# Strassen blocks in the feed-forward of a two-layer trunk, one weight sum of each block made by an adding DMA

## The chip, the core and the metric

One core of one Trainium2 chip runs the whole program. The time is the device time of one launch in microseconds, and of several launches the median. Engines are called as in the profile: PE is TensorE (PEld its weight loads), DVE is VectorE, ACT is ScalarE, POOL is GpSimd, SP is SyncE, which issues nearly all DMAs.

## What is computed

Two layers over 256 rows of 1024 numbers, all in float32. Each layer is a half-step SwiGLU feed-forward, a mixer (convolution branch, latent attention, gates, one output projection), and a second half-step feed-forward. The change is in the feed-forward, of which the program holds four (two in each layer):

```python
D_MODEL = 1024; SEQ = 256; DEPTH = 2; D_FF = 2816
def _swiglu(h, w_gate, w_up, w_down):
    return (jax.nn.silu(h @ w_gate) * (h @ w_up)) @ w_down
...
    for l in range(DEPTH):
        x = x + 0.5 * _swiglu(_rms_norm(x, ffn1_norm[l]), ffn1_w_gate[l], ffn1_w_up[l], ffn1_w_down[l])
        h = _rms_norm(x, mix_norm[l])
        ...
        x = x + y @ w_out[l]
        x = x + 0.5 * _swiglu(_rms_norm(x, ffn2_norm[l]), ffn2_w_gate[l], ffn2_w_up[l], ffn2_w_down[l])
    return x
```

## The kernel before, in words

**Split operands.** PE works on fp32r operands, and each float32 operand is kept as two of them: a rounded part ("hi") and what the rounding left ("lo"). A product is three matmuls (`products`, L663 to L665): hi by hi, hi by lo, lo by hi. For a weight block, ACT makes the hi part (`split` on ACT, L1123, raw to whi) and DVE the lo part (`split` on DVE, L1517, raw minus whi to wlo).

**Units.** Weights come in units of 128 by 2048 numbers (1 MB). `raw` holds three of them as they land, `whi` and `wlo` hold six (RING). SP loads a unit with two DMAs (`place`) when DVE has made the lo part of the unit three places earlier, ACT splits it when PE has released the unit six places earlier (`unit_free`), DVE follows ACT (`whi_ready`), and PE waits for DVE (`wlo_ready`). GpSimd takes DVE's part in a stretch of the mixer.

**Feed-forward.** The 2816 hidden columns are cut in 11 chunks of 256. For chunk c, `gate_up(c, t)` multiplies the 128 rows of tile t by 256 gate and 256 up columns side by side, over 8 blocks of 128 inner rows: 24 matmuls of 128x512 for each of two tiles, from two units. ACT applies silu to the gate half (L1216), DVE multiplies by the up half (`mul`, L1623) into `gu`. This must be transposed for the down product: ACT sorts the 32-bit words into 16-bit planes (`split_planes`, L1225), SP issues a DMA transpose (`plane_turn`, L402), DVE joins the planes again (`join`, L1636) into `g_turned`, ACT rounds that to gThi (`round_joined`, L1233) and DVE makes gTlo (`rest_joined`, L1522). Then `down(c, t)` adds chunk c to the output with 12 matmuls for each tile, from one unit, and waits for gTlo (`glo`). PE's order is gate_up(c), down(c-2), so a chunk is 72 matmuls. Chunks 4 and later run in a hardware loop on PE, chunks 2 and later on ACT and DVE.

**What sets the order.** Each engine runs the list that is written out for it, in order, and waits on semaphores. Nothing is moved by a scheduler. An instruction that waits holds up all that is written behind it on its engine, and SP's DMAs too are issued in the written order.

**GpSimd** computes inverse roots for the norms (`root`, L531) and, once in each layer, the angles for the rotary positions (L549 to L588, 36 counted steps), which ACT needs at the start of the mixer (L1321).

## Time and profile before

| | |
|---|---|
| median of 3 runs | 1047.45 us (1047.15 to 1047.8) |
| span of the profiled execution | 1045.7 us |
| PE busy | 1040.6 us |
| DVE, ACT, POOL busy | 687.1, 593.7, 248.9 us |
| granted TensorE clock | 1.000, the upper of its two levels |
| DMA | 208.81 MB, mean 200 GB/s |

The span is 1.75 us below the median of the times. In the page, the busy time of each engine tells which is always at work, the digits by slice tell whether that changes along the span, and the chain that ended last names the engine whose work the end waited for. A start and a duration in a timeline row overlap with the next row by some 0.1 us, since an engine begins an instruction while the one before it drains. So the cost of one instruction in a row of many is the distance between two starts.

### The profile page before, as it was taken

Reading aid. Unit: us, or ns where it says so; the run is one execution under the profiler, and the core shown is the slowest. Engines: PE = TensorE matmul, PEld = TensorE weight load, DVE = VectorE, ACT = ScalarE, POOL = GpSimd, SP = SyncE. Lnnn points to the kernel's source line nnn. Section 1 sums busy time; section 2 is a strip of 40 time slices with the busy share of each in tenths; the row PEclk is TensorE's granted clock in tenths of the full one; section 3 lists DMA queues with packets and bytes.
Section 4 is the critical chain, followed back from the end, with each engine's and each line's share of the span. In section 5 each row is a group of like instructions: output and inputs, shape, how many; then the busy total and the mean of one; then the engine's idle time right before and its main releaser. Section 6 shows DMA issues by size and latency. Waiting matters only on the chain.

```text
span 1045.7 us, 13767 instructions
## 1 busy us (share of the span) xinstructions
PE 1040.6 (100%) x5001; PEld 872.2 (83%) x5001; DVE 687.1 (66%) x911; ACT 593.7 (57%) x792; POOL 248.9 (24%) x258
## 2 busy tenths in 40 slices
PE   9999999999999999999999999999999999999998
PEld 6888888998888888888888888889988888888887
DVE  6755655698976766555576555656999677656551
ACT  6754544576874665445466454536778557645440
POOL 2960000148850000000048300002588300000000
PEclk9999999999999999999999999999999999999999
DMA  8977666455644696675569667565366366976641
GB/s 280 310 237 234 186 211 200 143 200 172 210 163 125 206 313 188 206 232 196 153 191 282 216 206 228 184 199 172 122 212 224 118 191 222 261 221 186 207 139 41
DMA packets 191555, 208.81 MB, mean 200 GB/s; under 512 B 64112, under 2 KB 162704, under 8 KB 191504
## 3 DMA queue, kind: packets, MB, share of 16 engines
q1 hardware_dynamic: 190288, 206.03, 63.6%
q10 hardware_dynamic: 1216, 2.11, 0.7%
q8 instruction: 31, 0.51, 0.2%
q14 instruction: 20, 0.16, 0.1%
HBM read 192.90 MB, written 1.05 MB: 185 GB/s over the span
## 4 chain that ended last, share of the span: by engine, by line
PE 98%; ACT 1%; DVE 1%; issue 0%; POOL 0%; ACTq 0%
PE bank L663 31%; PE bank L665 31%; PE bank L664 31%; PE bank L744 1%; PE bank L905 1%; PE bank L914 1%; PE bank L935 1%; PE bank L670 1%; PE bank L702 0%; PE bank L913 0%; PE bank L937 0%; DVE htok L1563 0%; DVE x L1611 0%; ACT htok L1132 0%; PE bank L923 0%; PE bank L963 0%
## 5 line engine op out<-in xcount | busy, mean ns | idle before, releaser
L1517 DVE TENSOR_TENSOR wlo<-raw,whi 128x2048 fp32r<-128x2048 f32 (+2 forms) x152 | 347.4, 2290 | 82.6 <-ACT whi L1123 81.5
L663 PE MATMUL bank<-whi,hThi 128*128 128x512 f32 (+1 forms) x976 | 378.4, 388 | 0.0
L665 PE MATMUL bank<-whi,hTlo 128*128 128x512 f32 (+1 forms) x976 | 373.7, 383 | 0.0
L664 PE MATMUL bank<-wlo,hThi 128*128 128x512 f32 (+1 forms) x976 | 373.6, 383 | 0.0
L1123 ACT ACTIVATE whi<-raw 128x2048 fp32r<-128x2048 f32 (+2 forms) x176 | 335.3, 1910 | 16.8 <-DMA raw<-in_ffn_w_up 7.3
L665 PEld LDWEIGHTS bank<-whi,hTlo 128*128 128x128 f32 x976 | 183.3, 188 | 35.7
L663 PEld LDWEIGHTS bank<-whi,hThi 128*128 128x128 f32 x976 | 183.4, 188 | 35.1 <-issue 0.3
L664 PEld LDWEIGHTS bank<-wlo,hThi 128*128 128x128 f32 x976 | 183.4, 188 | 34.8
L1216 ACT ACTIVATE gates<-bank,small 128x256 f32<-128x256 f32 x88 | 41.8, 475 | 263.5 <-PE bank L665 262.8
L663 PE MATMUL bank<-whi,gThi 128*128 128x512 f32 (+1 forms) x416 | 162.2, 390 | 0.0
L664 PE MATMUL bank<-wlo,gThi 128*128 128x512 f32 (+1 forms) x416 | 161.1, 387 | 0.0
L665 PE MATMUL bank<-whi,gTlo 128*128 128x512 f32 (+1 forms) x416 | 161.1, 387 | 0.0
L531 POOL TENSOR_TENSOR small<-small,expo 128x1 f32<-128x1 f32 (+3 forms) x20 | 24.2, 1214 | 566.3 <-DVE small L1556 529.5
L1623 DVE SCALAR_TENSOR_TENSOR gates<-bank,small,gates 128x256 f32<-128x256 f32 x88 | 42.4, 483 | 168.1 <-ACT gates L1216 168.0
L645 POOL TENSOR_TENSOR wlo<-raw,whi 128x2048 fp32r<-128x2048 f32 x24 | 110.2, 4612 | 21.9 <-ACT whi L1123 21.9
L1717 DVE SCALAR_TENSOR_TENSOR bank<-cu,vec,bank 128x256 f32<-128x256 f32 x240 | 98.1, 479 | 0.2
L665 PEld LDWEIGHTS bank<-whi,gTlo 128*128 128x128 f32 x416 | 78.1, 188 | 16.0
L663 PEld LDWEIGHTS bank<-whi,gThi 128*128 128x128 f32 x416 | 78.1, 188 | 15.8 <-issue 0.4
L664 PEld LDWEIGHTS bank<-wlo,gThi 128*128 128x128 f32 x416 | 78.2, 188 | 15.5
L1225 ACT ACTIVATE qkT<-gates 128x512 uint16<-128x512 uint16 x80 | 49.5, 620 | 0.0
L549 POOL TENSOR_TENSOR small<-expo 128x1 f32<-128x1 f32 x72 | 36.5, 507 | 5.9
L663 PE MATMUL bank<-hThi,whi 128*128 128x256 f32 x128 | 36.4, 284 | 0.0
(177 smaller groups left out, 823.6 us busy)
## 6 DMA issues: line engine op xcount, KB each, us to landing
raw<-in_ffn_w_down SPq DMA_DIRECT2D x88, 512.0 KB, 4.2
raw<-in_ffn_w_gate SPq DMA_DIRECT2D x84, 512.0 KB, 4.3
raw<-in_ffn_w_up SPq DMA_DIRECT2D x84, 512.0 KB, 5.4
raw<-in_w_in SPq DMA_DIRECT2D x48, 512.0 KB, 4.8
raw<-in_w_out SPq DMA_DIRECT2D x16, 512.0 KB, 4.4
raw<-in_w_in SPq DMA_DIRECT2D x8, 544.0 KB, 4.5
raw<-in_w_mla_out SPq DMA_DIRECT2D x8, 512.0 KB, 3.9
raw<-in_w_conv_out SPq DMA_DIRECT2D x8, 512.0 KB, 4.7
```

The source lines that it names most:

```text
L531: return nc.gpsimd.tensor_tensor(out, in_, expo[:, :].to_broadcast([P, out.shape[-1]]), ALU.pow)
L549: nc.gpsimd.tensor_tensor(small[:, 95:96], expo[:, :], expo[:, :], ALU.mult)
L645: nc.gpsimd.tensor_tensor(wlo[:, slot(u, RING), 0:n], raw[:, slot(u, RAW), 0:n], whi[:, slot(u, RING), 0:n].bitcast(F32), ALU.subtract).th ...
L663: nc.tensor.matmul(out, lh, rh, start=start, stop=False, skip_group_check=skip)
L664: nc.tensor.matmul(out, lh, rl, start=False, stop=False, skip_group_check=skip)
L665: return nc.tensor.matmul(out, ll, rh, start=False, stop=stop, skip_group_check=skip)
L1123: nc.scalar.activation(whi[:, slot(u0, RING), 0:USED[u0]], raw[:, slot(u0, RAW), 0:USED[u0]], ACT.Copy).then_inc(whi_ready, 1)
L1216: nc.scalar.activation(sgate[:, t, :], gu_bank(c, t)[:, 0:FC], ACT.Silu, scale=rs[:, t:t + 1]).then_inc(silu_ready, 1)
L1225: nc.scalar.activation(planes[:, :, :, t, :], words, ACT.Copy).then_inc(planes_ready, 1)
L1517: nc.vector.tensor_tensor(wlo[:, slot(u0, RING), 0:n], raw[:, slot(u0, RAW), 0:n], whi[:, slot(u0, RING), 0:n].bitcast(F32), ALU.subtract) ...
L1623: nc.vector.scalar_tensor_tensor(out=gu[:, t, :], in0=gu_bank(c, t)[:, FC:2 * FC], scalar=rs[:, t:t + 1], in1=sgate[:, t, :], op0=ALU.mult ...
L1717: ins = nc.vector.scalar_tensor_tensor(out=o, in0=i, scalar=w, in1=o, op0=ALU.mult, op1=ALU.add)
```

## The change

In each feed-forward, the chunks 3 and 4, and the chunks 6 and 7, form a block (BLK). A block is a product of a 2 by 2 matrix (row tiles t by inner halves h) with a 2 by 2 matrix (inner halves by gate and up, each 512 columns wide). It is computed with seven products of 12 matmuls in place of eight, by Winograd's form of Strassen's method. The products are called by their right operand: B11, T1, T2, B22, B21, T3, T4. The left operands are hT itself or one of four sums of its quarters (`mixed_rows`), made and split once in each feed-forward into sThi and sTlo. The right operands are the quarters of the weights or sums of them:

- `chain[0]` (in `htok`) is loaded by SP with the upper half of gate, which is B11. DVE adds to it three times, 128x2048 each: the upper half of up (`add_T1`, gives T1), the lower half of up (`add_T2`, gives T2), the lower half of gate (`add_T4`, gives T4). B22 and B21 are those lower halves of up and gate, loaded into `raw`.
- T3 is made in `chain[1]` (in `heads`): SP loads the upper half of up there, and an adding DMA issued by GpSimd (`add_rows`) adds the lower half of up from memory, in two parts of 512 KB.

The PSUM results are combined in `kept`: ACT copies four (`keep`), DVE makes four combinations of 128x512 (`up_first`, `gate_first`, `up_second`, `gate_second`), ACT applies silu twice at 128x512 and DVE multiplies twice at 128x512. Each of the seven right operands is a unit in the ring of six, with a hi part from ACT and a lo part from DVE, so that two chunks have 7 + 2 such splits where they had 4 + 2. The plain chunks stay as they were, but all loops are written out. `gain`, `bias`, `vtok` and `cu` of the mixer now share their room with sThi and sTlo, and `g_turned` has moved into `gates`. The core of the diff:

```diff
+BLK = (3, 6)
+PRODUCTS = ("B11", "T1", "D0", "T2", "B22", "B21", "T3", "T4", "D1")
...
+            def chain_load(l, f, c, i):
...
+                for k in (0, 2):
+                    sp.dma_start(dst[:, k:k + 2, :], src[:, k:k + 2, :]).then_inc(chain_landed[i], 16)
...
+            def add_rows(l, f, c):
+
+                done = per_block(l, f, c)
+                pool.wait_ge(chain_landed[1], done * 32)
+                pool.wait_ge(sum_ready, (done - 1) * 3 + 1)
...
+                for k in (0, 2):
+                    nc.gpsimd.dma_start(dst[:, k:k + 2, :], src[:, k:k + 2, :], accum_op=ALU.add).then_inc(added_landed, 16)
...
             for l in range(DEPTH):
                 norm(l, 0)
+                for c in BLK:
+                    add_rows(l, 0, c)
...
+                def block_product(c, name, b, lhs, start=True, stop=True):
+
+                    u = unit_block(f, c, name)
+                    unit_waits(pe, l, u)
+                    for k in range(4):
+                        ins = products(bank[:, b, :], lhs(k), wt(u, 2048, 4, k, slice(0, CW)),
+                                       start=start and k == 0, stop=stop and k == 3, skip=True)
+                    ins.then_inc(unit_free, 1)
...
+                    block_product(c, "B11", 4, plain_T(0, 0))
...
+                    block_product(c, "T1", 5, mixed_T(1, 1))
+                    down(c - 2, 0)
+                    down(c - 2, 1)
...
+                    block_product(c, "T2", 4, mixed_T(0, 0), start=False)
...
+                    block_product(c, "B22", 5, mixed_T(1, 0), start=False)
...
+                    block_product(c, "B21", 6, plain_T(1, 0))
...
+                    block_product(c, "T3", 4, mixed_T(0, 1), start=False)
...
+                    block_product(c, "T4", 7, plain_T(1, 1))
+                    down(c - 1, 0)
+                    down(c - 1, 1)
...
                 first()
-                pair(2, 2)
-                pair(3, 3)
-                with pe.Fori(0, (NCH - 5) // 2) as i:
-                    pair(i * 2 + 4, 4)
-                    pair(i * 2 + 5, 5)
+                pair(2)
+                strassen(3)
+                pair(5)
+                strassen(6)
+                pair(8)
+                pair(9)
                 last()
...
+                def mixed_round():
+
+                    act.wait_ge(mix_step, (l * 2 + f + 1) * 5)
+                    nc.scalar.activation(sThi[:, :, :], mixed, ACT.Copy).then_inc(mixed_hi, 1)
...
+                def add(c, i, other):
+
+                    nc.vector.tensor_tensor(chain[i], chain[i], other, ALU.add).then_inc(sum_ready, 1)
```

**VectorE at the start of the second feed-forward.** Before, from its third weight split on (L1517 the split, L1623 `mul`, L1636 `join`, L1522 `rest_joined`):

```order
L1517 TENSOR_TENSOR wlo<-raw,whi 128x2048 [waits whi_ready]
L1623 SCALAR_TENSOR_TENSOR gates<-bank,small,gates 128x256 [waits rs_ready,silu_ready]
L1517 TENSOR_TENSOR wlo<-raw,whi 128x2048 [waits whi_ready] x2
L1623 SCALAR_TENSOR_TENSOR gates<-bank,small,gates 128x256 [waits planes_ready,silu_ready]
L1636 COPY vtok<-qkT 128x2x512 [waits turned_landed]
L1517 TENSOR_TENSOR wlo<-raw,whi 128x2048 [waits whi_ready]
L1522 TENSOR_TENSOR gTlo<-vtok,gThi 128x512 [waits ghi]
L1623 SCALAR_TENSOR_TENSOR gates<-bank,small,gates 128x256 [waits planes_ready,silu_ready]
L1517 TENSOR_TENSOR wlo<-raw,whi 128x2048 [waits whi_ready]
```

The same place now, from the first row that is new, in two pieces (L2021 the sums of hT, L1854 a weight split, L1978 `join`, L1963 `mul`, L1861 `rest_joined` or the split of the sums, L2001 `add_T1` and `add_T2`):

```order
L2021 TENSOR_TENSOR gates<-hThi,hTlo 128x2048 [waits nlo,nhi]
L1963 SCALAR_TENSOR_TENSOR gates<-bank,small,gates 128x256 [waits planes_ready,silu_ready]
L2021 TENSOR_TENSOR gates<-gates 128x4x128 [waits mix_step]
L2021 TENSOR_TENSOR gates<-gates 128x4x128
L2021 TENSOR_TENSOR gates<-gates 128x4x128 [waits mix_step] x2
L1854 TENSOR_TENSOR wlo<-raw,whi 128x2048 [waits whi_ready]
L1978 COPY gates<-qkT 128x2x512 [waits turned_landed]
L1963 SCALAR_TENSOR_TENSOR gates<-bank,small,gates 128x256 [waits planes_ready,silu_ready]
L1861 TENSOR_TENSOR gTlo<-gates,gThi 128x512 [waits ghi]
```

```order
L1854 TENSOR_TENSOR wlo<-htok,whi 128x2048 [waits whi_ready]
L2001 TENSOR_TENSOR htok<-htok,heads 128x2048 [waits chain_landed1]
L1963 SCALAR_TENSOR_TENSOR gates<-bank,small,gates 128x256 [waits planes_ready,silu_ready]
L1861 TENSOR_TENSOR sTlo<-gates,sThi 128x2048 [waits mixed_hi]
L1963 SCALAR_TENSOR_TENSOR gates<-bank,small,gates 128x256 [waits planes_ready,silu_ready]
L1854 TENSOR_TENSOR wlo<-htok,whi 128x2048 [waits whi_ready]
L1978 COPY gates<-qkT 128x2x512 [waits glo,turned_landed]
L2001 TENSOR_TENSOR htok<-htok,raw 128x2048 [waits raw_landed1]
L1861 TENSOR_TENSOR gTlo<-gates,gThi 128x512 [waits ghi]
L1854 TENSOR_TENSOR wlo<-raw,whi 128x2048 [waits whi_ready]
```

Between two `mul` rows stood one or two weight splits. Now there stand the sums of hT, the adds and the split of the sums beside them, and the last row is the lo part of D1, the unit that `down(1)` needs.

**ScalarE at the same place.** Before (L1225 planes, L1123 weight split, L1216 silu, L1233 `round_joined`):

```order
L1225 ACTIVATE qkT<-gates 128x4x128 [waits gu_ready]
L1123 ACTIVATE whi<-raw 128x2048 [waits unit_free,raw_landed2]
L1216 ACTIVATE gates<-bank,small 128x256 [waits gu_done]
L1123 ACTIVATE whi<-raw 128x2048 [waits unit_free,raw_landed0]
L1233 ACTIVATE gThi<-vtok 128x512 [waits joined]
L1225 ACTIVATE qkT<-gates 128x4x128 [waits turned_landed,gu_ready]
L1216 ACTIVATE gates<-bank,small 128x256 [waits unit_free]
```

and now (L1503 planes, L1350 weight split, L1447 silu, L1511 `round_joined`, L1495 `mixed_round`):

```order
L1447 ACTIVATE gates<-bank,small 128x256 [waits gu_done]
L1350 ACTIVATE whi<-htok 128x2048 [waits unit_free,chain_landed0]
L1503 ACTIVATE qkT<-gates 128x4x128 [waits turned_landed,gu_ready]
L1511 ACTIVATE gThi<-gates 128x512 [waits joined]
L1495 ACTIVATE sThi<-gates 128x2048 [waits mix_step]
L1447 ACTIVATE gates<-bank,small 128x256 [waits unit_free]
L1503 ACTIVATE qkT<-gates 128x4x128 [waits gu_ready]
L1350 ACTIVATE whi<-htok 128x2048 [waits unit_free,sum_ready]
L1447 ACTIVATE gates<-bank,small 128x256 [waits gu_done]
```

The silu of chunk 1, tile 1 now stands behind `round_joined(0)` and `mixed_round`, and the silu of chunk 2, tile 0 behind the hi part of T1, which waits for `add_T1`.

**SyncE at the same place.** Before, the first transpose of a chunk (L402) stood right behind the loads of one down unit:

```order
L377 DMA raw<-in_ffn_w_gate 128x4x256 [waits wlo_ready]
L377 DMA raw<-in_ffn_w_up 128x4x256
L377 DMA raw<-in_ffn_w_down 128x1024 [waits wlo_ready]
L377 DMA raw<-in_ffn_w_down 128x1024
L402 DMA_TRANSPOSE qkT<-qkT 128x8x128 [waits joined,planes_ready]
```

and now:

```order
L469 DMA raw<-in_ffn_w_down 128x1024 [waits wlo_ready]
L469 DMA raw<-in_ffn_w_down 128x1024
L498 DMA htok<-in_ffn_w_gate 128x2x512 [waits sq_ready]
L498 DMA htok<-in_ffn_w_gate 128x2x512
L469 DMA raw<-in_ffn_w_down 128x1024 [waits wlo_ready]
L469 DMA raw<-in_ffn_w_down 128x1024
L498 DMA heads<-in_ffn_w_up 128x2x512 [waits block_joined1]
L498 DMA heads<-in_ffn_w_up 128x2x512
L469 DMA raw<-in_ffn_w_up 128x2x512 [waits wlo_ready]
L469 DMA raw<-in_ffn_w_up 128x2x512
L522 DMA_TRANSPOSE qkT<-qkT 128x8x128 [waits joined,planes_ready]
```

Five units (D0, chain[0], D1, chain[1], B22) are issued between the last unit of chunk 2 and the transpose of chunk 0, where one was.

## Rows read from the trace of the kernel before

**Rows 1.** The page: engines, busy by slice, and the chain that ended last

```profile
PE 1040.6 (100%) x5001; PEld 872.2 (83%) x5001; DVE 687.1 (66%) x911; ACT 593.7 (57%) x792; POOL 248.9 (24%) x258
PE   9999999999999999999999999999999999999998
PE 98%; ACT 1%; DVE 1%; issue 0%; POOL 0%; ACTq 0%
```

**Rows 2.** Timeline, ScalarE, second feed-forward: start, us, engine, line, instruction, [idle before]

```profile
353.64 1.97 ACT L1123 ACTIVATE whi<-raw 128x2048 fp32r<-128x2048 f32 x1
355.45 0.67 ACT L1225 ACTIVATE qkT<-gates 128x512 uint16<-128x512 uint16 x1
357.04 0.47 ACT L1216 ACTIVATE gates<-bank,small 128x256 f32<-128x256 f32 x1 [0.92 <-PE bank L665]
357.41 1.91 ACT L1123 ACTIVATE whi<-raw 128x2048 fp32r<-128x2048 f32 x1
...
360.14 1.92 ACT L1123 ACTIVATE whi<-raw 128x2048 fp32r<-128x2048 f32 x1 [0.30 <-DMA raw<-in_ffn_w_up]
...
373.36 0.47 ACT L1216 ACTIVATE gates<-bank,small 128x256 f32<-128x256 f32 x1 [0.69 <-PE bank L665]
...
378.80 0.47 ACT L1216 ACTIVATE gates<-bank,small 128x256 f32<-128x256 f32 x1 [1.41 <-PE bank L665]
```

**Rows 3.** Timeline, VectorE, same stretch

```profile
352.44 2.29 DVE L1517 TENSOR_TENSOR wlo<-raw,whi 128x2048 fp32r<-128x2048 f32 x1 [0.67 <-ACT whi L1123]
354.65 0.48 DVE L1623 SCALAR_TENSOR_TENSOR gates<-bank,small,gates 128x256 f32<-128x256 f32 x1
...
355.64 2.29 DVE L1517 TENSOR_TENSOR wlo<-raw,whi 128x2048 fp32r<-128x2048 f32 x1 [0.45 <-ACT whi L1123]
357.85 0.48 DVE L1623 SCALAR_TENSOR_TENSOR gates<-bank,small,gates 128x256 f32<-128x256 f32 x1
...
364.70 0.75 DVE L1636 COPY vtok<-qkT 128x1024 uint16<-128x1024 uint16 x1
365.33 2.28 DVE L1517 TENSOR_TENSOR wlo<-raw,whi 128x2048 fp32r<-128x2048 f32 x1
```

**Rows 4.** The page's groups: plain weight splits and the operations of 128x512 on each engine

```profile
L1517 DVE TENSOR_TENSOR wlo<-raw,whi 128x2048 fp32r<-128x2048 f32 (+2 forms) x152 | 347.4, 2290 | 82.6 <-ACT whi L1123 81.5
L1522 DVE TENSOR_TENSOR gTlo<-vtok,gThi 128x512 fp32r<-128x512 f32 x40 | 27.4, 686 | 3.3 <-ACT gThi L1233 3.3
L1233 ACT ACTIVATE gThi<-vtok 128x512 fp32r<-128x512 f32 x40 | 24.9, 622 | 18.1 <-DVE vtok L1636 17.6 <-PE bank L665 0.5
```

**Rows 5.** Timeline, SyncE's queue, second feed-forward

```profile
354.76 0.37 SPq L377 DMA_DIRECT2D raw<-in_ffn_w_gate  x1
355.17 0.51 SPq L377 DMA_DIRECT2D raw<-in_ffn_w_up  x1
357.96 0.82 SPq L377 DMA_DIRECT2D raw<-in_ffn_w_down  x2
359.86 1.23 SPq L402 DMA_TRANSPOSE qkT<-qkT  x1
```

**Rows 6.** The page: DMA issues, KB each, median us from issue to landing

```profile
raw<-in_ffn_w_gate SPq DMA_DIRECT2D x84, 512.0 KB, 4.3
raw<-in_ffn_w_up SPq DMA_DIRECT2D x84, 512.0 KB, 5.4
```

**Rows 7.** Two transposes by themselves: behind a down unit's loads at 37.0, behind none

```profile
L402 SPq DMA_TRANSPOSE qkT<-qkT x1: 1232/1232/1232, 37.0 to 37.0; - x1
...
DMA to landing us min/median/max: 5.1/5.1/5.1
...
L402 SPq DMA_TRANSPOSE qkT<-qkT x1: 1232/1232/1232, 62.8 to 62.8; - x1
...
DMA to landing us min/median/max: 3.0/3.0/3.0
```

**Rows 8.** By window: us, busy of PE, PEld, DVE, ACT, POOL, clock, DMA share, GB/s

```profile
22.30:72.90 50.60, 50.60 (x224) 41.72 (x223) 35.91 (x29) 32.39 (x34) 45.53 (x88) 1.00 1.00 293
...
26.00:52.00 26.00, 26.00 (x116) 21.33 (x115) 20.40 (x16) 18.76 (x19) 23.77 (x37) 1.00 1.11 313
...
346.00:400.00 54.00, 54.00 (x244) 44.83 (x243) 37.62 (x37) 36.64 (x42) 0.57 (x1) 1.00 0.79 240
```

**Rows 9.** Timeline, GpSimd: two angle steps of layer 1, then first and last of layer 0

```profile
578.56 2.14 POOL L549 TENSOR_TENSOR small<-expo 128x1 f32<-128x1 f32 x1
...
580.76 2.35 POOL L568 TENSOR_SCALAR ang<-ang 128x32 f32<-128x32 f32 x1
...
23.70 11.63 POOL L556 TENSOR_SCALAR ang<-small 128x2 f32<-128x2 f32 x16
...
67.51 0.20 POOL L549 TENSOR_TENSOR small<-expo 128x1 f32<-128x1 f32 x1
...
72.29 0.57 POOL L549 TENSOR_TENSOR small<-expo 128x1 f32<-128x1 f32 x1
```

**Rows 10.** Timeline, VectorE, beside the first two of rows 9

```profile
578.35 4.62 DVE L1517 TENSOR_TENSOR wlo<-raw,whi 128x2048 fp32r<-128x2048 f32 x2 [1.23 <-ACT whi L1123]
```

**Rows 11.** Timeline, ScalarE: where layer 0's mixer takes the angles

```profile
202.31 0.34 ACT L1321 ACTIVATE cossin<-ang 128x32 f32<-128x32 f32 x2
```

More of the change, by code:

```diff
@@ L61 @@
 UM = U_FFN
-assert U_LAYER % RING == 0 and U_LAYER % RAW == 0
+assert U_LAYER % RING == 0
+LOADED = [u for f in range(2) for u in range(UB[f], UB[f] + U_FFN)
+          if FFN_UNITS[u - UB[f]][0] in ("G0", "G1", "D", "B22", "B21")] + list(range(UM, UM + U_MIX))
+LOADED.sort()
+R_LAYER = len(LOADED)
+PLAIN = [c for c in range(NCH) if not any(b <= c < b + 2 for b in BLK)]
 M_PR, M_C01, M_UQ, M_UKV, M_C23, M_G, M_MLA, M_CO, M_WO = 0, 2, 4, 5, 6, 8, 16, 18, 20
@@ L808, in turn, with down @@
                     ins.then_inc(gtr, 1)
-                def down(c, c0, t, last=False, between=None):
+                def down(c, t, last=False, between=None):
                     pe.wait_ge(glo, per_ffn(l, f, c, t))
@@ new lines, in ffn @@
+                silu(1, 0)
+                first_of(3, "B11")
+                split_planes(1, 0)
+                round_joined(0)
+                mixed_round()
+                silu(1, 1)
+                split_planes(1, 1)
+                sum_of(3, "T1")
+                silu(2, 0)
+                down_split(1)
+                split_planes(2, 0)
+                silu(2, 1)
+                round_joined(1)
+                split_planes(2, 1)
+                block_first(3)
+                block_second(3)
@@ new lines, in ffn @@
+                    gate_split(2, 0)
+                    gate_split(2, 1)
+                    mul(0, 1)
+                whole_rows()
+                mul(1, 0)
+                mixed_rows()
+                down_split(0)
+                join(0)
+                mul(1, 1)
+                rest_joined(0)
+                of_chain(3, "B11")
+                add_T1(3)
+                mul(2, 0)
+                mixed_rest()
+                mul(2, 1)
+                of_chain(3, "T1")
+                join(1)
@@ new lines, in ffn @@
+                add_T2(3)
+                rest_joined(1)
+                down_split(1)
+                of_chain(3, "T2")
+                add_T4(3)
+                join(2)
+                lower(3, "B22")
+                lower(3, "B21")
+                rest_joined(2)
+                of_chain(3, "T3")
+                of_chain(3, "T4")
+                block_second(3)
+                of_chain(6, "B11")
+                add_T1(6)
+                join(3)
+                rest_joined(3)
+                mul(5, 0)
@@ new lines, in ffn @@
+                of_chain(6, "T1")
+                join(4)
+                add_T2(6)
+                mul(5, 1)
+                rest_joined(4)
+                down_split(4)
+                of_chain(6, "T2")
+                add_T4(6)
+                lower(6, "B22")
+                join(5)
+                lower(6, "B21")
+                rest_joined(5)
+                of_chain(6, "T3")
+                of_chain(6, "T4")
+                block_second(6)
+                gate_split(9, 0)
+                join(6)
```

588 lines of the change are left out of this document (445 added, 143 removed).

## The prediction

> **What bounds the kernel now.** I read the engines' busy time first, then the chain that ended last, then the timelines of one feed-forward. PE is busy for 1040.6 of 1045.7 us, at nine tenths or more in all slices but the last, and it is 98% of the chain [rows 1]. So fewer matmuls make the kernel faster, as long as nothing that PE waits for gets later than its lead. From one silu of ScalarE to the next of the same chunk lie one tile's 24 matmuls: 378.80 - 373.36 = 5.44 us [rows 2], or 0.2267 us for a matmul of 128x512. In that stretch VectorE is busy for 37.6 of 54 us and ScalarE for 36.6 [rows 8].
>
> **What is removed.** Each block takes 7 x 12 matmuls where two chunks took 96. That is 12 fewer, 8 blocks, 96 x 0.2267 = **21.8 us** off PE. All of it lies on the path.
>
> **What is added on VectorE.** A split of 128x2048 costs 2.21 us from start to start (352.44 to 354.65), `mul` 0.40, `join` 0.63 (364.70 to 365.33) [rows 3]; an operation of 128x512 lasts 0.686 [rows 4], less some 0.08 of overlap 0.61. The trace has no add of two SBUF tiles, but the split is such an operation, with two SBUF inputs of the same size and another operator. I take 2.21 for an add (bounds 2.2 and 2.3). A block has 3 more splits and 3 adds, 13.3 us, and the combinations (4 x 0.61) and two wide for four narrow multiplies (1.22 - 1.60) bring it to 15.3. Two blocks and the sums of hT (2.21 + 4 x 0.61 + 2.21 = 6.9) make 37.5 us more in each feed-forward. ScalarE gets 3 more splits of 1.81 (353.64 to 355.45 [rows 2]) and four copies of about 0.52 (0.622 long [rows 4]) in each block, and one more split for the sums.
>
> On the average this fits. A block lasts 144 - 12 = 132 matmuls, 29.9 us, and VectorE's work in it is 9 x 2.21 + 3 x 2.21 + 2.4 + 1.2 + 2 x (0.63 + 0.61) = 32.6 us, while a plain chunk leaves it 16.3 - 8.7 = 7.6 us free. The ring of six units carries the lack of 2.7 us. The question is the order, and the tightest place is the first block of a feed-forward.
>
> **The walk to D1.** I use the clock of the trace in the second feed-forward [rows 2, 3, 5]; the lists are those in the section on the change. Up to VectorE's second split the lists agree. The split of the second unit of chunk 2 can't begin before 362.0: its load is issued when the first split has ended (354.76 [rows 5]) and it lands at 360.1, where ScalarE takes it today too [rows 2]. That split ends at 364.2, and `mul(0,1)`, done today at 358.2 [rows 3], at 364.6. From there VectorE has until D1's lo part is done: three adds or sums of 2.21 (the whole of hT, `add_T1`, `add_T2`), four of 0.61, the split of the sums, three splits (D0, B11, T1), and D1's (together 8 x 2.21 = 17.7), 2.4, four `mul` 1.6, two joins and two rests 2.5. That is 24.2 us, and ends at 388.8.
>
> PE comes to D1 at 378.8 (end of chunk 2) + 5.44 (down(0)) + 2 x 2.72 (B11, T1) = **389.7**. So without any wait VectorE would be there 0.9 us ahead. It has these waits, each a wait for ScalarE or a DMA that stands in line:
> - `mul(1,0)` for its silu, which ScalarE reaches behind D0's hi part: 0.6.
> - `join(0)` for the transpose. VectorE comes to it at 372.6. The transpose is issued at about 365.5 behind five units, 5.24 MB, whose issue begins at 358.0. The second DMA of a unit is issued 0.41 us after the first [rows 5] and lands 5.4 - 4.3 = 1.1 us later after its own issue [rows 6], so 524 KB take 1.5 us, 350 GB/s; over 26 us the queue moved 313 GB/s at a full share [rows 8]. 5.24 MB at 350 take 15 us from about 360.2. The transpose waits for loads ahead of it: 5.1 us with one down unit before it against 3.0 with none [rows 7]. It lands at 375.5, and VectorE waits 2.9. Bounds: 0 if transposes pass loads, 5 at 313 GB/s.
> - `mul(1,1)` for its silu, which now stands behind `round_joined(0)` (0.52) and `mixed_round` (1.81): with hand-overs 2.8.
> - `mul(2,0)` for its silu, behind T1's hi part, which waits for `add_T1`: 1.81 + 0.35 = 2.2. PE had those products done long before.
> - four small hand-overs, 0.4 in all.
>
> Together 8.9 us, so D1 is ready at 388.8 + 8.9 = 397.7, **8.0 us** after PE wants it. PE meets them in pieces: 1.2 at down(0), 1.7 at B11 (bank 4 is free only after `mul(2,0)`), 2.1 at T1, 3.0 at D1. Behind D1, VectorE stays ahead: T2, `add_T4`, join, B22 end at 405.0, and PE, with D1 from 397.7, wants T2 at 403.1 and B22 at 405.9.
>
> **The rest of a feed-forward.** VectorE ends T4 at 412.2 (after B21, a rest and T3). From there to the end of `rest_joined(3)` it has 6 x 2.21 + 7 x 0.61 + 0.63 = 18.2 us of work, and waits of 3.7: `up_second` for a `keep` that stands behind a silu (1.3), the second multiply for a silu behind D3's hi part (1.3), B11 (0.4), the round (0.7). That is 434.1. PE ends T4 at 403.1 + 5 x 2.72 = 416.7 and wants down(3) at 416.7 + 5.4 + 10.9 = 433.0: **1 us** late. To the second block's T4 VectorE has some 41 us of work for PE's 204 matmuls, 46.2 us, and stays ahead. Then the transpose of chunk 6 stands in SyncE's list behind both units of chunk 9, the second of which waits for the second split of chunk 8; I have it issued 1.7 us into gate_up(8). From there: 5.5 to land (between the two of rows 7 and more), two `split_planes` and a round on ScalarE 1.6, the hi and lo parts of chunk 9's second unit 1.8 + 2.2, since `rest_joined(6)` stands behind them, that rest 0.6: 13.4 us after gate_up(8) began, which lasts 10.9: **2.5 us** late. In the first feed-forward the queue is already full (share 1.11 [rows 8]), so `join(0)` waits some 2.5 us longer.
>
> **The sum.** 1045.7 - 21.8 + 4 x (8.0 + 1.0 + 2.5) + 2.5 = 1072.4, against the profile's own span. The median lies 1.75 above the span, so I predict **1074 us**, slower by 2.5%.
>
> The Trainium skill (DMA: Bandwidth & Descriptors, Queues, rings and completion order) says that each engine consumes the descriptors of one queue in ring order, and that another queue is served in turns. The transpose rows agree. By it the adding DMA, on GpSimd's queue, slows the transposes but doesn't stand before them, and the sum stays as it is.
>
> **What else moves and costs nothing.** The memset of `cu` (128x120) and the later load of `gain` lie under matmuls with slack of tens of us. The loops written out bring more instruction loads, in a queue with 0.2% of the DMA engines' time. The clock stood at its upper level throughout [rows 8]; I leave it there, as waits of 1 to 3 us between runs of matmuls are short.
>
> **Rivals.**
> 1. *VectorE keeps its lead.* If the hand-overs on ScalarE are covered and the transpose passes the loads, PE sees next to nothing, and the time is 1047.5 - 21.8 = 1025.7 to 1035. For it: the free 0.9 us of the walk, and the 7.6 us free in each plain chunk. Against: the two silus stand in ScalarE's list behind the waits, and no speed of DMA removes those 5.0 us.
> 2. *Only the queue is better than I think.* Without the wait for `join(0)` and with quick transposes the first block is 5.1 late, and chunks 3 and 6 together about 0.5, as the transpose is some 2 us sooner: 4 x 5.6 = 22 against 21.8, so 1048, within 1041 to 1053.
> 3. *The adding DMA, or GpSimd behind it, is late.* ScalarE needs T3's sum some 17 us after `add_T1`, VectorE 21 us after; the two plain loads of a unit take 5.9 (0.5 of issue and 5.4 [rows 6]). So the adding DMA decides when it is more than about three times slower than a load, and then each us costs one in each of 8 blocks: at 5 us over, 1074 + 40 = 1114. No row shows an adding DMA. The same engine starts the angles only after the second block's add, at about 106 us, not 23.7 [rows 9]. A GpSimd operation of 0.20 us lasts 2.14 beside a split, and of two splits back to back each lets one operation through [rows 9, 10]. The angles are 88 instructions [rows 8] from 23.7 to 72.9; where nothing holds them, 18 take 72.29 - 67.51 = 4.8 us [rows 9], so all take 23.5. Some 25 splits and adds between 106 and the mixer, 55 us, and 23.5 of their own end at 185, against ScalarE's need at 202.3 [rows 11] plus delays. It holds, with little room, and would cost 5 to 15 us in each layer if not.
>
> The Trainium skill (SBUF — State Buffer, Who interferes with whom) has this as a rule: a VectorE instruction with two SBUF inputs contends with a GpSimd instruction that reads SBUF, and the later one blocks. The trace agrees (2.14 against 0.20).
>
> **How the numbers follow.** The forecast (PE waits 9 to 16 us in each feed-forward) has 0.61 and its own range of 1058 to 1090; rival 2 has 0.14, rival 1 0.13, rival 3 0.12. The range of 1041 to 1098 leaves out rival 1 and half of rival 3, 0.19. A measurement of this kernel can tell 0.2% (2 us) from no change. Faster: rival 1 and 0.07 of rival 2, 0.20. The same: 0.05. Slower: 0.75.
>
> **What would show it.** Right: PE idle 10 to 13 us in each feed-forward, with waits at the down products of chunks 0, 3 and 6, at B11, T1 and D1 of the first block; VectorE idle before `join(0)` and before the multiplies of chunks 1 and 2, "released by ACT gates"; transposes that land 8 to 10 us after issue; PE busy about 1019. Wrong: transposes of 3 us beside queued loads, or VectorE with no gap before those rows; an adding DMA of over 17 us; ScalarE waiting for `added_landed` or for the angles.

## The result, and the profile after

| | before | after |
|---|---|---|
| median, us | 1047.3 (1047.02 to 1047.8, 4 runs) | 1089.66 (1085.8 to 1090.2, 4 runs) |
| span of the profiled execution | 1045.7 | 1088.4 |
| PE busy | 1040.6 | 1041.4 |
| PE idle (span less busy) | 5.1 | 47.0 |
| granted clock, mean | 1.00 | 0.984 |

The changed kernel takes 1.0398 times as long (95% interval 1.0386 to 1.0411): 42.4 us more, where the forecast was 26.7 more. The page has these engines, and this clock in 40 slices:

```profile
PE 1041.4 (96%) x4905; PEld 863.9 (79%) x4905; DVE 830.4 (76%) x1000; ACT 660.1 (61%) x836; POOL 293.7 (27%) x274
PEclk9899999999999999999999999999999999899999
```

PE has the 96 matmuls fewer (against [rows 1]), and yet it is as busy as before. The list of waits shows the idle time (engine, line, waited for: us in total, times, longest):

```profile
PE bank L833 <- DVE gTlo L1861: 22.2, 10, 3.2
PE bank L833 <- DVE wlo L1854: 15.8, 8, 2.7
PE bank L833 <- DVE gates L1963: 2.9, 2, 1.5
```

These three rows are 40.9 us, and all of it is released by VectorE: lo parts of gated values (at the down products), lo parts of weights (at T1 and D1), multiplies (at B11). What else the list has is 2.3 us, nearly all of it in the first 13 us of the program. PE's timeline of the second feed-forward has the six places one by one, with the wait at the end of the row; in order they are the down products of chunk 0, B11, T1, D1, and the down products of chunks 3 and 6:

```profile
393.02 0.50 PE L833 MATMUL bank<-whi,gThi 128*128 128x512 f32 x1 [1.37 <-DVE gTlo L1861]
400.25 0.50 PE L833 MATMUL bank<-whi,hThi 128*128 128x512 f32 x1 [1.46 <-DVE gates L1963]
405.22 0.47 PE L833 MATMUL bank<-whi,sThi 128*128 128x512 f32 x1 [1.96 <-DVE wlo L1854]
410.86 0.47 PE L833 MATMUL bank<-whi,gThi 128*128 128x512 f32 x1 [1.06 <-DVE wlo L1854]
448.38 0.50 PE L833 MATMUL bank<-whi,gThi 128*128 128x512 f32 x1 [1.89 <-DVE gTlo L1861]
497.68 0.64 PE L833 MATMUL bank<-whi,gThi 128*128 128x512 f32 x1 [2.76 <-DVE gTlo L1861]
```

What the forecast did not have stands behind the last of these waits. PE's timeline (start, duration):

```profile
494.52 0.39 PE L835 MATMUL bank<-whi,hTlo 128*128 128x512 f32 x1
497.68 0.64 PE L833 MATMUL bank<-whi,gThi 128*128 128x512 f32 x1 [2.76 <-DVE gTlo L1861]
...
500.67 0.63 PE L834 MATMUL bank<-wlo,gThi 128*128 128x512 f32 x1
501.10 0.49 PE L835 MATMUL bank<-whi,gTlo 128*128 128x512 f32 x1
501.43 0.40 PE L833 MATMUL bank<-whi,gThi 128*128 128x512 f32 x1
501.66 0.40 PE L834 MATMUL bank<-wlo,gThi 128*128 128x512 f32 x1
```

From start to start a matmul takes 0.43 us here, and from 501.43 on 0.23 again. There are eight such stretches in the trace. By window (us, busy of PE, clock, DMA share, GB/s), four of them:

```profile
48.80:54.30 5.50, 5.50 (x15) 0.51 0.25 48
405.80:409.20 3.40, 3.40 (x10) 0.51 0.82 118
497.70:501.40 3.70, 3.70 (x9) 0.54 0.84 255
949.70:955.20 5.50, 5.50 (x14) 0.50 0.54 194
```

The granted clock is at its lower level, 1.2 GHz, for 3 to 6 us of matmuls each time. I took the time between the starts of neighbouring matmuls over the whole trace behind the start of the program and summed what exceeds 0.2267 us. In gaps over 0.5 us that is 46.2 us: 22 waits, two of them under 0.25 us, and four intervals right behind a wait, in which the first matmul at the lower clock took 0.54 to 0.59 us (1.4 us in all, so a part of the clock's price stands among the waits). In intervals of 0.3 to 0.5 us it is 22.2 us, against 6.6 in the trace before: **15.6 us of slow matmuls**. So 1045.7 - 21.8 + 46.2 + 15.6 = 1085.7 of the 1088.4. Of the 2.7 left, 1.3 is ahead of the first wait (PE starts the same matmul at 39.6 us before and at 40.9 now), and 1.4 I can't assign.

### The profile page after: what moved, and what is told of

It is laid out like the page before. It is cut to its first block and busy times, and to the rows that moved or that the text cites. A ratio compares the mean times of both kernels' runs of the same rounds, so it can differ in the third digit from the quotient of the medians.

```text
span 1088.4 us, 13247 instructions
## 1 busy us (share of the span) xinstructions
PE 1041.4 (96%) x4905; PEld 863.9 (79%) x4905; DVE 830.4 (76%) x1000; ACT 660.1 (61%) x836; POOL 293.7 (27%) x274
## 5 line engine op out<-in xcount | busy, mean ns | idle before, releaser
L1854 DVE TENSOR_TENSOR wlo<-raw,whi 128x2048 fp32r<-128x2048 f32 (+2 forms) x136 | 308.9, 2283 | 50.8 <-ACT whi L1350 50.6
L1350 ACT ACTIVATE whi<-raw 128x2048 fp32r<-128x2048 f32 (+2 forms) x160 | 303.1, 1910 | 48.5 <-DMA raw<-in_ffn_w_up 34.4
L833 PE MATMUL bank<-whi,hThi 128*128 128x512 f32 (+1 forms) x816 | 316.5, 388 | 2.9 <-DVE gates L1963 2.9
L835 PE MATMUL bank<-whi,hTlo 128*128 128x512 f32 (+1 forms) x816 | 311.4, 382 | 0.0
L834 PE MATMUL bank<-wlo,hThi 128*128 128x512 f32 (+1 forms) x816 | 311.3, 382 | 0.0
L833 PE MATMUL bank<-whi,gThi 128*128 128x512 f32 (+1 forms) x416 | 170.0, 409 | 31.5 <-DVE gTlo L1861 22.2
L833 PEld LDWEIGHTS bank<-whi,hThi 128*128 128x128 f32 x816 | 153.3, 188 | 32.6 <-DVE gates L1963 4.1
L835 PEld LDWEIGHTS bank<-whi,hTlo 128*128 128x128 f32 x816 | 153.2, 188 | 29.8
L1503 ACT ACTIVATE qkT<-gates 128x512 uint16<-128x512 uint16 x80 | 49.3, 626 | 102.9 <-DMA qkT<-qkT 45.6
L2212 DVE SCALAR_TENSOR_TENSOR bank<-shared,vec,bank 128x256 f32<-128x256 f32 x240 | 98.1, 479 | 0.2
L1350 ACT ACTIVATE whi<-htok 128x2048 fp32r<-128x2048 f32 x32 | 61.1, 1910 | 21.7 <-DVE htok L2001 21.3
L1854 DVE TENSOR_TENSOR wlo<-htok,whi 128x2048 fp32r<-128x2048 f32 x32 | 73.0, 2282 | 1.2 <-ACT whi L1350 1.2
L1963 DVE SCALAR_TENSOR_TENSOR gates<-bank,small,gates 128x256 f32<-128x256 f32 x56 | 26.9, 481 | 55.2 <-ACT gates L1447 55.0
```

The costliest lines, as they stand in the source:

```text
L833: nc.tensor.matmul(out, lh, rh, start=start, stop=False, skip_group_check=skip)
L834: nc.tensor.matmul(out, lh, rl, start=False, stop=False, skip_group_check=skip)
L835: return nc.tensor.matmul(out, ll, rh, start=False, stop=stop, skip_group_check=skip)
L1350: nc.scalar.activation(whi[:, slot(u, RING), 0:USED[u]], src, ACT.Copy).then_inc(whi_ready, 1)
L1503: nc.scalar.activation(planes[:, :, :, t, :], words, ACT.Copy).then_inc(planes_ready, 1)
L1854: nc.vector.tensor_tensor(wlo[:, slot(u, RING), 0:n], src, whi[:, slot(u, RING), 0:n].bitcast(F32), ALU.subtract).then_inc(wlo_ready, 1)
```

## The experiments

"Waits" in this table is the span less PE's busy time, "slow" the excess of intervals of 0.3 to 0.5 us over the 6.6 of before. Medians are of 4 runs, and of 10 to 12 for loops_out and where the text says five rounds. The 2.6 of busy_waits, at a clock of 1.00, is the first interval behind each run of zeros, 0.33 us long.

| kernel | median | span | waits | slow | clock |
|---|---|---|---|---|---|
| before | 1047.3 | 1045.7 | 5.1 | 0 | 1.00 |
| changed | 1089.7 | 1088.4 | 47.0 | 15.6 | 0.984 |
| loops_out | 1047.4 | 1045.6 | 6.5 | 0 | 1.00 |
| waits_put_in | 1085.5 | 1083.4 | 33.6 | 7.7 | 0.987 |
| busy_waits | 1082.2 | 1081.2 | 17.7 | 2.6 | 1.00 |
| silu_first | 1076.2 | 1077.5 | 40.2 | 12.6 | 0.986 |
| rests_first | 1073.1 | 1071.7 | 38.2 | 10.5 | 0.989 |
| both_orders | 1063.7 | 1061.0 | 31.8 | 7.0 | 0.991 |
| fill_b11 | 1053.9 | 1051.9 | 25.4 | 5.1 | 0.995 |
| third_silu | 1047.0 | 1044.4 | 17.7 | 7.0 | 0.993 |
| third_busy | 1045.9 | 1043.2 | 8.0 | 0.9 | 1.00 |
| room_made | 1048.3 | 1041.7 | 18.3 | 2.8 | 0.998 |
| sum_on_vector | 1105.4 | 1103.1 | 59.6 | 18.4 | 0.981 |
| turn_queue | 1088.9 | 1086.5 | 45.4 | 18.1 | 0.983 |

### The slow matmuls: is it PE's waiting, the longer program, or something else?

> The kernel before with its three loops over chunks written out, as the changed kernel has them, and nothing else. Theory (the 16 us that my forecast lacked are matmuls at the lower clock behind PE's waits): no wait, no change, 1045 to 1050 us, granted clock 1.00. Rival (the longer program itself costs, by instruction loads): 1055 to 1063 us.

```
-                with pe.Fori(0, (NCH - 5) // 2) as i:
-                    pair(i * 2 + 4, 4)
-                    pair(i * 2 + 5, 5)
+                for c in range(4, NCH - 1):
+                    pair(c, c)
...
```

The loops of ScalarE and VectorE are written out in the same way. 1047.36 us, ratio 1.0002 (0.9993 to 1.0012): the written-out loops cost nothing.

> The kernel before with its loops written out and ten waits of PE put in: in each of the two second feed-forwards PE waits, ahead of the down products of five chunks, for a chain of 2, 4, 6, 9 and 12 small operations on GpSimd that begins when the products ahead have ended. At some 0.5 us for an operation the waits are about 1, 2, 3, 4.5 and 6 us, 33 us in all. Theory (a wait of PE of some 3 us brings its clock down for the matmuls behind it, whatever the cause of the wait): the granted clock falls behind the longer waits and stands at 1.00 behind the shortest, and the time is the kernel before plus the waits plus 1.3 to 2.6 us for each wait of 3 us and more, 1088 to 1096 us. Rival (the slow matmuls of the changed kernel have another cause than its waits): clock 1.00 throughout, time the kernel before plus the waits alone, 1080 us.

```
+HOLDS = ((3, 2), (5, 4), (6, 6), (8, 9), (9, 12))
...
+                for i, (c, n) in enumerate(HOLDS):
+                    unit_released(pool, l, unit_gu(1, c, 1))
+                    for j in range(n):
+                        held[0] += 1
+                        nc.gpsimd.tensor_tensor(small[:, 95:96], expo[:, :], expo[:, :], ALU.mult).then_inc(hold_step, 1)
+                        pool.wait_ge(hold_step, held[0])
+                    pool.sem_inc(hold_done, 1)
...
+                    if f == 1 and c in [h for h, _ in HOLDS]:
+                        pe.wait_ge(hold_done, l * len(HOLDS) + [h for h, _ in HOLDS].index(c) + 1)
                     down(c - 2, c0 - 2, 0)
```

1085.54 us (ratio 1.0369, 1.0352 to 1.0387). The waits came out at 0.65, 1.20, 1.75, 2.57 and 7.7 us, twice each. This is PE's timeline around a wait of 2.57, and then the windows behind waits of 0.65, 1.75, 2.57 and 7.7:

```profile
1018.38 0.50 PE L676 MATMUL bank<-whi,gThi 128*128 128x512 f32 x1 [2.57 <-POOLq L668]
1018.72 0.55 PE L677 MATMUL bank<-wlo,gThi 128*128 128x512 f32 x1
1019.07 0.63 PE L678 MATMUL bank<-whi,gTlo 128*128 128x512 f32 x1
```

```profile
930.60:934.00 3.40, 3.40 (x16) 1.00 0.77 284
983.00:986.00 3.00, 3.00 (x14) 1.00 0.84 280
1018.60:1022.00 3.40, 3.40 (x9) 0.53 0.86 189
1045.00:1049.50 4.50, 4.50 (x12) 0.50 0.02 4
```

The clock fell behind all four waits of 2.57 us and more, and behind none of the six shorter ones. There is no Strassen block in this kernel, so a wait is enough. 30.5 us of gaps and 7.7 of slow matmuls are the 38.2 us by which it is longer than loops_out. The time is 2.5 us below the range that I gave: the waits came out 2.5 us shorter in all than the 33 us expected, and four of them were long enough for a fall, where I had six.

> The changed kernel, with products of zeros put ahead of the places where PE waits (8 ahead of the down products of chunk 0, 6 ahead of B11, 8 ahead of T1, 6, 7 and 11 ahead of the down products of chunks 1, 3 and 6), so that PE works in about the time in which it waited. They add zero, and nothing else is changed. Theory (idle PE brings the clock down): the clock stays at 1.00 or near it, the runs of 7 to 13 matmuls at 0.42 us are gone, and the time is 1088 less about 14 us, plus 1 to 4 for zeros that last longer than the wait they fill: 1073 to 1080 us. Rival (the clock falls for another reason): the slow runs stay, 1087 to 1094 us.

```
                     else:
+                        stay_busy(6)
                         pe.wait_ge(gu_ready, per_gu(l, f, 2, 0))
                     block_product(c, "B11", 4, plain_T(0, 0))
...
                     else:
+                        stay_busy(8)
                         pe.wait_ge(gu_ready, per_gu(l, f, 2, 1))
...
+                    if t == 0 and c == 0:
+                        keep_busy(8)
+                    elif t == 0 and c in (1, 3, 6):
+                        stay_busy({1: 6, 3: 7, 6: 11}[c])
                     pe.wait_ge(glo, per_ffn(l, f, c, t))
```

1082.18 us, clock 1.00. In PE's timeline the zeros stand where the waits were:

```profile
390.76 1.90 PE L840 MATMUL bank<-zero 128*128 128x512 bf16 x8
392.68 0.50 PE L833 MATMUL bank<-whi,gThi 128*128 128x512 f32 x1
...
398.26 1.47 PE L845 MATMUL bank<-zero 128*128 128x512 bf16 x6
399.90 0.50 PE L833 MATMUL bank<-whi,hThi 128*128 128x512 f32 x1 [0.18 <-DVE gates L1975]
```

Two zeros more last 1.90 - 1.47 = 0.43 us, so the 184 take 39.6. PE's other busy time is 1063.5 - 39.6 = 1023.9, against 1041.4 in the changed kernel: 17.5 us less, and every stretch of slow matmuls is gone. The gain in time is only 7.5 us, 2 short of the range I gave, since the zeros and the waits left (39.6 + 17.7 = 57.3) last 10.3 us longer than the 47.0 of waits that they replace. The rival is out. PE's idle time brings the clock down, and not the products of the blocks.

### The waits: what stands in line ahead of what VectorE needs?

VectorE's timeline in the changed kernel has the waits that the prediction named, ahead of `join(0)`, `mul(1,1)` and `mul(2,0)`; ScalarE's shows why, and SyncE's queue the transpose:

```profile
383.55 2.29 DVE L1854 TENSOR_TENSOR wlo<-raw,whi 128x2048 fp32r<-128x2048 f32 x1
388.20 0.76 DVE L1978 COPY gates<-qkT 128x1024 uint16<-128x1024 uint16 x1 [2.36 <-DMA qkT<-qkT]
391.88 0.48 DVE L1963 SCALAR_TENSOR_TENSOR gates<-bank,small,gates 128x256 f32<-128x256 f32 x1 [2.92 <-ACT gates L1447]
...
399.71 0.48 DVE L1963 SCALAR_TENSOR_TENSOR gates<-bank,small,gates 128x256 f32<-128x256 f32 x1 [2.34 <-ACT gates L1447]
```

```profile
388.26 0.63 ACT L1503 ACTIVATE qkT<-gates 128x512 uint16<-128x512 uint16 x1 [5.86 <-DMA qkT<-qkT]
389.05 0.63 ACT L1511 ACTIVATE gThi<-gates 128x512 fp32r<-128x512 f32 x1 [0.16 <-DVE gates L1978]
389.59 1.90 ACT L1495 ACTIVATE sThi<-gates 128x2048 fp32r<-128x2048 f32 x1
391.40 0.45 ACT L1447 ACTIVATE gates<-bank,small 128x256 f32<-128x256 f32 x1
...
397.40 1.91 ACT L1350 ACTIVATE whi<-htok 128x2048 fp32r<-128x2048 f32 x1 [4.37 <-DVE htok L2001]
399.22 0.45 ACT L1447 ACTIVATE gates<-bank,small 128x256 f32<-128x256 f32 x1
```

```profile
378.45 5.34 SPq L522 DMA_TRANSPOSE qkT<-qkT  x1
```

> The changed kernel, with ScalarE's silu(1,1) ahead of split_planes(1,0), round_joined(0) and mixed_round, silu(2,0) ahead of T1's hi part, and VectorE's mul(1,1) ahead of join(0). Theory (these two silus stand in line behind waits, and VectorE waits 2.9 and 2.3 us for them, while its lateness is what PE meets): the two waits are gone, some 3 us less of PE's waits in each feed-forward, and a fall of the clock or two less: 1071 to 1081 us. Rival (the transpose of chunk 0, which lands 9.7 us after its issue, sets it all, and VectorE only waits for it instead): 1085 us or more.

```
                 first_of(3, "B11")
+                silu(1, 1)
                 split_planes(1, 0)
                 round_joined(0)
                 mixed_round()
-                silu(1, 1)
                 split_planes(1, 1)
+                silu(2, 0)
                 sum_of(3, "T1")
-                silu(2, 0)
...
+                mul(1, 1)
                 join(0)
-                mul(1, 1)
```

1076.16 us (ratio 1.0268, 1.025 to 1.0287), 13.5 less than the changed kernel. The waits at the down products of chunk 0 and at B11 are gone but in the first feed-forward (0.88 at the former); T1 took part of what they held, with 2.1 to 3.4 us, since VectorE now waits 2.07 us at `mul(2,1)` for a third silu. So PE's waits fell by 6.8 us in all, 1.7 in each feed-forward, where I had 3, and the clock still fell eight times. (The profile is of the slowest of the four runs, 3.2 us above their median.)

> The changed kernel, with two rests of VectorE moved ahead: join(3) and rest_joined(3) ahead of add_T1(6), and rest_joined(6) ahead of chunk 9's second split. Theory (PE's waits at the down products of chunks 3 and 6, some 1.9 and 2.8 us in each feed-forward, come from what stands ahead of these rests, and each fall of the clock at chunk 6 goes with its wait): 1069 to 1079 us, with a wait of up to 1.7 us at T1 or D1 of the second block in their place. Rival (VectorE is short of time as a whole, and the wait only moves to the units behind): 1083 us or more.

```
                 of_chain(6, "B11")
-                add_T1(6)
                 join(3)
                 rest_joined(3)
+                add_T1(6)
...
                 join(6)
+                rest_joined(6)
                 gate_split(9, 1)
-                rest_joined(6)
```

1073.06 us (ratio 1.0244, 1.0227 to 1.0261): 16.6 less. PE no longer waits at the down products of chunks 3 and 6. In their place it waits 0.3 to 2.1 us for D4's lo part, in three of four feed-forwards, with no fall of the clock.

> The orders of silu_first and rests_first together in the changed kernel. Theory (the terms add, since they lie 50 us apart): 1076 less 10 to 19, so 1057 to 1066 us. Rival (what is left of the lateness and of the clock's falls is shared, and the sum is much smaller): 1068 us or more.

The edit is the two above. 1063.73 us (ratio 1.0172, 1.0148 to 1.0196): 25.9 less than the changed kernel, of 13.5 + 16.6 = 30.1. They nearly add.

> As both_orders, and VectorE makes the lo part of B11 ahead of join(0), in the time in which it waits for the transpose of chunk 0. Theory (that wait of 2.4 to 3 us, made by the transpose behind five units in the queue, is passed on to T1 and D1): the wait at T1 is gone or under 1 us, that at D1 stays at 1.5 to 3 us as VectorE has 5.6 us of work between the lo parts of T1 and D1 for PE's 2.7, 4 x 2.2 us and two or three falls less than both_orders: 1044 to 1056 us. Rival (B11's lo part ahead of the rest of chunk 0 makes PE wait at down(0) instead): within 3 us of both_orders.

Against both_orders:

```
                 mul(1, 1)
+                of_chain(3, "B11")
                 join(0)
                 rest_joined(0)
-                of_chain(3, "B11")
                 add_T1(3)
```

1053.87 us (ratio 1.0077, 1.0048 to 1.0107), 9.9 less again. T1's wait is 0.4 to 1.2 us, D1's 2.6 to 2.9, as the theory has it. VectorE's timeline shows one more silu in line:

```profile
383.70 2.28 DVE L1861 TENSOR_TENSOR sTlo<-gates,sThi 128x2048 fp32r<-128x2048 f32 x1
388.05 0.49 DVE L1963 SCALAR_TENSOR_TENSOR gates<-bank,small,gates 128x256 f32<-128x256 f32 x1 [2.08 <-ACT gates L1447]
```

> As fill_b11, and ScalarE's silu(2,1) ahead of T1's hi part. In fill_b11 VectorE waits 2.1 us ahead of mul(2,1) for this silu, which stands behind the hi parts of T1 and D1, while PE has had its products done for 4 us. Theory (it is the last silu that stands in line; T1's lo part then is 2 us sooner, ahead of PE, and D1's wait falls from 2.9 to about 1 us, too short for a fall of the clock): 1054 less 4 x (0.9 + 1.8) less two or three falls of 1.5 us, 1037 to 1044 us, faster than the kernel before. Rival (T1's hi part, now behind two silus, is late itself, and D1's wait stays as VectorE has 5.6 us of work between T1 and D1): 1049 us or more.

Against fill_b11:

```
                 silu(2, 0)
+                silu(2, 1)
                 sum_of(3, "T1")
                 down_split(1)
                 split_planes(2, 0)
-                silu(2, 1)
```

1047.02 us in five rounds, ratio 1.0002 (0.9992 to 1.0012): as fast as the kernel before. T1's wait is gone, D1's is 1.3 to 1.9, D4's 0 to 2.1. I had D1's at about 1 us and too short for a fall; the clock still fell three times behind it and once behind D4's, so the time is 3 us above the range.

> As third_silu, with 8 products of zeros (1.8 us) put ahead of the down products of chunks 1 and 4, where PE still waits 0.4 to 2.1 us, 13.5 us in all, and where the four falls of the clock that are left begin. Theory (the clock falls for PE's idle time): the granted clock is 1.00, the four runs of 8 and 9 slow matmuls, 7 us together, are gone, and 1 to 4 us come back where the zeros last longer than the wait: 1041 to 1045 us. Rival (the falls stay whatever PE does there): 1047 us or more.

Against third_silu:

```
+                    if t == 0 and c in (1, 4):
+                        stay_busy(8)
                     pe.wait_ge(glo, per_ffn(l, f, c, t))
```

1045.91 us in five rounds, ratio 0.9989 (0.998 to 0.9997), clock 1.00. The same stretch by window, of third_silu and then of this kernel:

```profile
566.00:580.00 14.00, 12.20 (x48) 0.88 0.74 140
```

```profile
560.00:580.00 20.00, 19.91 (x89) 1.00 0.67 132
```

The falls are gone here as well, but the 64 zeros take 13.8 us where the waits fell by 9.7, so the gain is 1.1 us, and the time is 0.9 above the range. It is 0.1% better than the kernel before, less than the 0.2% that I set as the least to speak of.

> As third_silu, and in the three feed-forwards but the first VectorE makes the sum of all rows of hT ahead of the second split of chunk 2, for whose load it waits 2 us, and add_T1 ahead of join(0), for whose transpose it then would wait; ScalarE rounds the sums ahead of split_planes(1,0), where it waits 5 us for the same transpose. Theory (VectorE works from there to D1 without a gap, so 2 us that it waited come off D1's lateness in each of three feed-forwards): D1's waits of 1.3 to 1.9 us go, with up to three falls of the clock: 1047 less 5 to 11, 1036 to 1042 us. Rival (the transpose, which can't be earlier, is then what the down products of chunk 0 wait for, and nothing is won): 1045 us or more.

Against third_silu:

```
+                mixed_round()
                 split_planes(1, 0)
                 round_joined(0)
-                mixed_round()
...
                     gate_split(2, 0)
+                    whole_rows()
                     gate_split(2, 1)
...
                 of_chain(3, "B11")
+                if (l, f) != (0, 0):
+                    add_T1(3)
                 join(0)
                 rest_joined(0)
+                if (l, f) == (0, 0):
+                    add_T1(3)
```

1048.27 us in five rounds (1043.48 to 1050.62), ratio 1.001 (1.0002 to 1.0019): nothing won, as the rival says. The profile is of the fastest run. D1's waits are gone in the three feed-forwards, but PE waits 1.3 us at the down products of chunk 0 and 1.7 to 2.2 at D4, and VectorE, which now comes to `mul(1,0)` early, waits for its silu there:

```profile
367.51 0.48 DVE L1963 SCALAR_TENSOR_TENSOR gates<-bank,small,gates 128x256 f32<-128x256 f32 x1 [2.86 <-ACT gates L1447]
```

### The adding DMA against VectorE

> The changed kernel, with T3's sum made by VectorE: one add of 2.2 us from the loaded second unit, behind add_T4, in place of the adding DMA from GpSimd. Theory (VectorE is the engine that is late, so an add more is passed on to PE at the next place where it is late, chunk 3's down products or T3 itself in the first block and T1 or chunk 6 in the second): 4 to 5 us more in each feed-forward with the clock's falls, 1100 to 1112 us. Rival (behind D1 VectorE is ahead of PE and has room for 2.2 us; the adding DMA then buys nothing): 1085 to 1092 us.

```
                 add_T4(3)
+                add_T3(3)
...
-                for c in BLK:
-                    add_rows(l, 0, c)
```

1105.41 us (ratio 1.0555, 1.0538 to 1.0573), 15.8 more than with the adding DMA, 2.0 for each add, which lasts 2.28 us (8 adds, 18.3 us busy). Most of what VectorE gets is passed on to PE: its waits grow by 12.6 us and the slow matmuls by 2.8. In the changed kernel the page and GpSimd's timeline show what the DMA takes (the number after KB is the us to landing):

```profile
heads<-in_ffn_w_up POOLq DMA_DIRECT2D x16, 512.0 KB, 6.1
```

```profile
398.00 1.31 POOL L702 DMA_DIRECT2D heads<-in_ffn_w_up  x1 [29.29 <-DVE htok L2001]
404.39 1.47 POOL L702 DMA_DIRECT2D heads<-in_ffn_w_up  x1 [5.08 <-issue]
```

### The transpose and its place in the queue

> The changed kernel, with the transpose of chunk 0 issued by ScalarE on its own queue as soon as the planes are written, in place of SyncE, behind five units. Theory (it lands 9.7 us after its issue as it stands in line behind 5.2 MB of loads, and on another queue it passes them): it lands in 3 to 6 us, VectorE's wait of 2.4 us ahead of join(0) is gone, and the time is 1088 less 6 to 13 us: 1075 to 1082 us. Rival (the DMA engines are full, and the transpose is as slow in any queue, or ScalarE loses by the issue what VectorE gains): 1086 us or more.

```
+                act.wait_ge(planes_ready, per_turn(l, f, 0) * TT)
+                act.wait_ge(joined, per_turn(l, f, 0))
+                act.dma_start_transpose(turned[:, :, :], planes.rearrange("p b k t f -> p (b k t f)")
+                                        ).then_inc(turned_landed, 16)
                 down_split(0)
...
                 lower_load(l, f, 3, "B22")
-                turn(0)
```

1088.92 us, ratio 1.0418 (1.0396 to 1.044): no gain over the changed kernel's 1.0398. The page's rows (us to landing at the end), then ScalarE's timeline at the second of the four, and VectorE's:

```profile
qkT<-qkT SPq DMA_TRANSPOSE x43, 3.6
qkT<-qkT ACTq DMA_TRANSPOSE x4, 10.5
```

```profile
374.37 1.28 ACTq L1570 DMA_TRANSPOSE qkT<-qkT  x1
375.75 1.92 ACT L1349 ACTIVATE whi<-raw 128x2048 fp32r<-128x2048 f32 x1 [1.41 <-issue]
...
378.06 0.48 DVE L1966 SCALAR_TENSOR_TENSOR gates<-bank,small,gates 128x256 f32<-128x256 f32 x1 [2.19 <-ACT gates L1446]
```

The theory fell. With nothing ahead of it in its own queue the transpose still takes 9.4 to 12.9 us (median 10.5). In the three later feed-forwards seven loads of 512 KB are on their way when it is issued, and it lands 0.2 to 0.3 us behind the last of them. The issue also keeps ScalarE idle for 1.41 us, and VectorE waits 2.19 (0.67 in the changed kernel) for silu(1,0), which stands behind it; its wait ahead of `join(0)` falls from 2.36 to 0.51 with that, and nothing is won. The transpose with the loads held back wasn't run for itself, but the changed kernel's trace has both ends: of its 40 transposes of chunks the nine issued with no load on its way land after 3.0 to 3.1 us, and the four with seven loads on their way after 9.0 to 10.5.

## The prediction, point by point

- **What bounds the kernel, and what is removed: right.** PE's waits in the changed kernel are released by VectorE, all but 0.9 us at the start of the program. third_busy, with hardly a wait and no fall, has PE busy for 1035.2 - 13.8 = 1021.4 us, 19.2 under the kernel before. The sum took off 21.8; the 2.6 between them is not assigned.
- **The walk to D1: right.** Forecast for the second feed-forward were PE waits of 1.2 at down(0), 1.7 at B11, 2.1 at T1, 3.0 at D1. From start to start, less 0.23, they are 1.5, 1.6, 2.1 and 1.2. At D1 the slow matmuls of T1 (8 in the window from 405.8, 1.6 us) had used up part of the wait. VectorE's waits were given as 2.9 at `join(0)` (2.36), 2.8 at `mul(1,1)` (2.92) and 2.2 at `mul(2,0)` (2.34). silu_first shows that the last two are waits in line.
- **Chunks 3 and 6:** forecast 1.0 and 2.5, measured 2.1 and 2.9. rests_first shows the cause that I gave, the work ahead of the two rests.
- **The sum of waits:** forecast 4 x 11.5 + 2.5 = 48.5, measured 12.2, 11.5, 12.2 and 10.0 in the four feed-forwards: 45.9. The 2.5 more of the first feed-forward were at its `join(0)`, where PE waits 3.2 us at down(0), but B11 has no wait there.
- **"I leave the clock there, as waits of 1 to 3 us between runs of matmuls are short": wrong.** This is the term that was mis-sized. I gave the clock nothing, and it costs 15.6 us in eight falls, 2 us each. It is nearly all of the 16.0 us that the forecast lacks: 1072.4 - 48.5 + 46.2 + 15.6 = 1085.7, of 1088.4. That the time still lies within the range of 1058 to 1090 is owed to the width of the range, since no term of the sum stood for the clock. The trace before has no wait of PE beyond the start, so its clock of 1.00 in every window [rows 8] could not tell what a wait does. A bound "up to one fall behind each wait" was to be put beside the zero.
- **The transpose:** forecast 10.0 us to landing, measured 9.7. The size was right, and its reason, the place in the ring, was not: turn_queue takes that place away and the transpose is as slow. What it goes with is the loads on their way, in whichever queue. The Trainium skill (DMA: Bandwidth & Descriptors, Queues, rings and completion order) states that another queue is served in turns. That the transpose would then pass the loads was my inference, and turn_queue doesn't bear it out.
- **Rival 1 (VectorE keeps its lead)** did not happen with this order. third_silu, with a few instructions moved, goes part of the way: 17.7 us of PE's idle time are left, and its 1047.0 us are still 12 above the rival's range. **Rival 2** (only the queue is better) is out, as the transpose took the 10 us that I gave it. **Rival 3 (the adding DMA late)** did not happen, by less than I thought. ScalarE wants T3's sum at 413.85. The second of its two DMAs is issued 6.4 us after the first and lands 6.1 us later, at 410.5, 13 us after `add_T1`; my window was 17. The angles of layer 0 ended at 172.5 where I had 185, and ScalarE took them at 215.2, with no wait for them in the list.
- **Signs:** the waits at the named places, VectorE's gaps "released by ACT gates" and transposes of 8 to 10 us were there. "PE busy about 1019" was not, and that alone pointed to the clock.

## What to carry to other kernels

When PE is the bound and an edit makes it wait, price two things: the wait, and the matmuls at the lower clock behind it. Here a wait of 2.6 us or more cost some 2 us on top in nearly every case, and one of 1.8 to 2.6 us in every second. Products of zeros in a known wait hold the clock and show at once how much of a loss it is, but they pay only where they last less beyond the wait than the slow matmuls cost (10.3 us against 17.5 in busy_waits, 4.1 against 5.3 in third_busy). An engine with 76% of its time busy can still be the one that is late: look in the lists of its helpers for short operations that it needs (here three silus of 0.45 us) which stand behind long ones that wait themselves; moving those three, a multiply, a split and two rests gave back 42.6 us.
